# A two-block transformer on one core: more blocks beside the first feed-forward's rows, modulation units begun later, weighted squares on ScalarE

## The reference

```python
mod = c_act @ w_ada[l] + b_ada[l]                       # 6 * 2048 values
sh_a, sc_a, gt_a, sh_f, sc_f, gt_f = split(mod, 6)
...
x = x + gt_a * mix                                      # mix = (...) @ w_o
h = _rmsnorm(x, norm_ffn[l]) * (1.0 + sc_f) + sh_f
gate, up = jnp.split(h @ w_gate_up[l], 2, axis=-1)      # 2 * 5632 columns
x = x + gt_f * ((jax.nn.silu(gate) * up) @ w_down[l])
return _rmsnorm(x, final_norm)                          # end of the first block
# second block
h = rms_norm(x, pre_mix_g[l])
proj = h @ w_in[l]
```

## Time and profile before

| | us |
|---|---|
| median of 3 runs | 2901.99 (2901.83 to 2907.34) |
| the profiled execution | 2915.39 |
| its span, first to last instruction | 2912.6 |
| PE busy | 2802.3 (96%) |
| DVE busy | 2045.2 (70%) |
| ACT busy | 1316.2 (45%) |
| POOL busy | 209.4 (7%) |

### The profile page before, as it was taken

One profiled execution on the slowest core, in us unless ns is written; L12 is line 12 of the kernel. 1 busy time (PEld: TensorE's weight loads), 2 busy tenths in 40 slices (PEclk: granted clock), 3 DMA queues, 4 the chain that ended last, 5 costly groups with the idle time before them and its releaser, 6 DMA issues.

```text
span 2912.6 us, 45616 instructions
## 1 busy us (share of the span) xinstructions
PE 2802.3 (96%) x18282; PEld 2512.9 (86%) x18282; DVE 2045.2 (70%) x3021; ACT 1316.2 (45%) x2033; POOL 209.4 (7%) x180
## 2 busy tenths in 40 slices
PE   6988999999999999999999999999999999999997
PEld 6987788999999888888888889888888888888886
DVE  7888885667687786555555688997557566565665
ACT  4445542332344544444444454344555444444454
POOL 0230000000001100000000080111110000000001
PEclk9999999999999999999999999999999999999999
DMA  9863255555688587555555555544445555555553
GB/s 392 315 217 130 95 171 177 189 188 180 206 311 280 198 296 243 182 188 187 188 186 183 188 174 174 167 152 137 146 131 177 185 187 188 182 187 188 187 187 126
DMA packets 158466, 565.40 MB, mean 194 GB/s; under 512 B 17584, under 2 KB 21936, under 8 KB 158256
## 3 DMA queue, kind: packets, MB, share of 16 engines
q1 hardware_dynamic: 158256, 562.50, 57.9%
HBM read 560.33 MB, written 2.10 MB: 193 GB/s over the span
## 4 chain that ended last, share of the span: by engine, by line
PE 84%; DVE 10%; ACT 3%; issue 2%; DMA 1%; SPq 0%; POOL 0%; DVEq 0%; ACTq 0%; POOLq 0%
PE BK L346 32%; PE BK L347 16%; PE BK L349 10%; PE BK L351 9%; PE BK L350 9%; DVE LO L623 2%; PE BK L431 2%; DVE ADA L619 1%; ACT HI L507 1%; DVE B L673 1%; DVE TV L718 1%; DVE B L830 1%; PE BK L356 1%; PE BK L474 1%; PE BK L479 1%
## 5 line engine op out<-in xcount | busy, mean ns | idle before, releaser
L346 PE MATMUL BK<-H,HI 128*128 128x512 f32 x4144 | 1466.3, 399 | 10.8 <-DVE LO L623 7.6
L507 ACT ACTIVATE HI<-RAW 128x1024 fp32r<-128x1024 f32 x825 | 874.1, 1060 | 1287.7 <-PE BK L347 721.9
L623 DVE TENSOR_TENSOR LO<-RAW,HI 128x1024 fp32r<-128x1024 f32 x825 | 1018.1, 1235 | 402.0 <-ACT HI L507 399.8
L347 PE MATMUL BK<-H,LO 128*128 128x256 f32 x4144 | 1162.8, 281 | 0.0
L346 PEld LDWEIGHTS BK<-H,HI 128*128 128x128 f32 x4144 | 780.4, 188 | 205.9 <-DVE LO L623 9.2
L349 PE MATMUL BK<-H,HI 128*128 128x256 f32 x2720 | 809.3, 298 | 35.3 <-DVE B L673 20.3
L347 PEld LDWEIGHTS BK<-H,LO 128*128 128x128 f32 x4144 | 784.2, 189 | 0.2
L350 PE MATMUL BK<-H,HI 128*128 128x256 f32 x2720 | 778.3, 286 | 0.0
L351 PE MATMUL BK<-H,LO 128*128 128x256 f32 x2720 | 777.9, 286 | 0.0
L349 PEld LDWEIGHTS BK<-H,HI 128*128 128x128 f32 x2720 | 530.0, 195 | 76.6 <-issue 36.7
L350 PEld LDWEIGHTS BK<-H,HI 128*128 128x128 f32 x2720 | 530.7, 195 | 1.5 <-issue 1.0
(11 more groups left out here) (234 smaller groups left out, 1693.6 us busy)
## 6 DMA issues: line engine op xcount, KB each, us to landing
RAW<-wst_dram SPq DMA_DIRECT2D x825, 512.0 KB, 3.4
RAW<-wada_dram SPq DMA_DIRECT2D x155, 512.0 KB, 4.5
EARLY<-wada_dram SPq DMA_DIRECT2D x37, 512.0 KB, 8.5
EARLY<-wst_dram SPq DMA_DIRECT2D x33, 512.0 KB, 6.8
X<-xT_dram SPq DMA_DIRECT2D x8, 512.0 KB, 8.9
B<-bias_dram SPq DMA_DIRECT2D x32, 128.0 KB, 3.4
out_dram<-X SPq DMA_DIRECT2D x3, 512.0 KB, 2.7
CN<-consts_dram SPq DMA_DIRECT2D x1, 840.0 KB, 9.0
```

Source lines behind the costliest of these rows:

```text
L346: e.matmul(bk[:, :], hh, H[:, k, :], start=first, stop=False, skip_group_check=True)
L347: e.matmul(bk[:, 256:512], ll, H[:, k, 0:256], start=False, stop=last, skip_group_check=True).then_inc(S["tile"], 1)
L507: e.activation(HI[:, u % NHL, :], raw_at(slot), ACT.Copy).then_inc(S["hi"], 1)
L623: e.tensor_tensor(LO[:, u % NHL, :], raw_at(slot), HI[:, u % NHL, :].bitcast(f32), sub).then_inc(S["lo"], 1)
```

## The change

Three edits. `first1` runs three pairs, six blocks, in place of two pairs. The A units after the 160th are due at 160 + (i - 238) * 3/4 in place of 160 + (i - 220) * 5/8, so they stand between L240 and L281 in place of L222 and L272. `scaled_square` is one ScalarE operation (Square with final_norm as scale) that writes SQ's second half, or ACC2 for row 0, and `scaled_add` on GpSimd adds it to ACC2.

```diff
--- before.py
+++ after.py
@@ -529,6 +529,10 @@
                 q.wait_ge(ready, free)
                 e.activation(dst, src, ACT.Square).then_inc(S["st_a"], 1)
 
+            def scaled_square(dst, j, x, free, before):
+                q.wait_ge(x, free, before)
+                e.activation(dst, X[:, j, :], ACT.Square, scale=col("final_norm", j)).then_inc(S["st_a"], 1)
+
             def gained(dst, src, scale, ready):
                 q.wait_ge(ready)
                 e.activation(dst, src, ACT.Copy, scale=scale).then_inc(S["ev_a"], 1)
@@ -592,7 +596,7 @@
                 e.activation(y, t, ACT.Tanh).then_inc(S["cv_a"], 1)
 
             walk(dict(c_sigmoid=c_sigmoid, hi=hi, copy_sum=copy_sum, split_hi=split_hi, tanh=tanh, sigmoid=sigmoid, square=square,
-                      gained=gained, root_table=root_table, root_guess=root_guess, sine=sine, beta=beta, softplus=softplus, gate_exp=gate_exp, row_square=row_square,
+                      gained=gained, scaled_square=scaled_square, root_table=root_table, root_guess=root_guess, sine=sine, beta=beta, softplus=softplus, gate_exp=gate_exp, row_square=row_square,
                       soft_exp=soft_exp, turned=turned, g_exp=g_exp, g_copy=g_copy, conv_square=conv_square, conv_tanh=conv_tanh))
 
         def vector(e):
@@ -865,15 +869,9 @@
                 q.wait_ge(square, free)
                 e.tensor_tensor(SQ[:, 0, :], SQ[:, 0, :], B3[:, 6 + p, :], add).then_inc(S["st_g"], 1)
 
-            def scaled_square(j, x, free, before, at):
-                q.wait_ge(x, free)
-                sq = SQ[:, 1, :]
-                e.tensor_scalar(sq, X[:, j, :], col("final_norm", j), None, mult).then_inc(S["st_g"], 1)
-                q.wait_ge(("st_g", at + 1), before)
-                e.tensor_tensor(ACC2 if j == 0 else sq, sq, sq, mult).then_inc(S["st_g"], 1)
-                if j:
-                    q.wait_ge(("st_g", at + 2))
-                    e.tensor_tensor(ACC2, ACC2, sq, add).then_inc(S["st_g"], 1)
+            def scaled_add(square, before):
+                q.wait_ge(square, before)
+                e.tensor_tensor(ACC2, ACC2, SQ[:, 1, :], add).then_inc(S["st_g"], 1)
 
             def bias_mask(i, loaded):
                 q.wait_ge(loaded)
@@ -883,7 +881,7 @@
                 q.wait_ge(copied)
                 e.tensor_tensor(dst, dst, t, add).then_inc(S["ev_g"], 1)
 
-            walk(dict(part_add=part_add, square_add=square_add, scaled_square=scaled_square, bias_mask=bias_mask))
+            walk(dict(part_add=part_add, square_add=square_add, scaled_add=scaled_add, bias_mask=bias_mask))
 
         def walk(mine, log=None):
             w = Walk(mine)
@@ -904,7 +902,7 @@
             put = 16 * GROUPS
             late_at = len(kinds) - 16
             for i in range(ERA * (GROUPS - 1), N_TILES // 8):
-                due = min(N_ADA, put if i < 80 else 64 + (i - 80) * 3 // 4 if i < 208 else 160 + (max(i, 220) - 220) * 5 // 8)
+                due = min(N_ADA, put if i < 80 else 64 + (i - 80) * 3 // 4 if i < 208 else 160 + (max(i, 238) - 238) * 3 // 4)
                 kinds += ["L"] + ["A"] * max(0, due - put)
                 put = max(put, due)
             lin_at = [i for i, k in enumerate(kinds) if k == "L"]
@@ -1872,8 +1870,8 @@
                     yield from blocks(H1, h_tok, 0, "w_gate_up", 0, [o], wide=True)
 
             def first1(f_tok):
-                run(blocks(H1, h_tok, 0, "w_gate_up", 0, up1_outs(0, 0, f_tok) + up1_outs(1, 1, f_tok), wide=True))
-                return 2
+                run(blocks(H1, h_tok, 0, "w_gate_up", 0, [o for i in range(3) for o in up1_outs(i, i, f_tok)], wide=True))
+                return 3
 
             h2_free = [mid]
             ST = Stats(Sp.done)
@@ -1888,7 +1886,8 @@
                     yield from f(bk, tok, own)
                     if ci < 2:
                         return
-                    acc2[0] = do("scaled_square", "st_g", j, x_tok[j], ST.before, acc2[0], n=3 if j else 2)
+                    k = do("scaled_square", "st_a", SQ[:, 1, :] if j else ACC2, j, x_tok[j], ST.before, acc2[0])
+                    acc2[0] = do("scaled_add", "st_g", k, acc2[0]) if j else k
                     ST.before = ST.before + [acc2[0]]
                     yield
                     u_tok2[j] = yield from split(H1, j, X[:, j, :], x_tok[j], [fp_tok, h1_done[0]], scale=FP[:, j:j + 1])
```

## The result

The change made the kernel slower. In runs taken in turns on one chip the changed kernel took 2923.41 us (median of 9, 2911.93 to 2929.77), the kernel before 2901.58 (median of 9, 2896.86 to 2917.62). The ratio is 1.0065 with a 95% interval of 1.0049 to 1.0082: some 19 us (the two medians differ by 21.8), where 9 were forecast. The sign was right. The time lies above the forecast's range, which ended at 2917.

A forecast was written before the change was run, and what follows sets the result against it. TensorE was taken as the bound, 84% of the chain of waits. −1.3 at the start of the first feed-forward and +10.1 in the third w_down pass made +8.8 on 2901.99: 2911 us, range 2901 to 2917.

The forecast's parts named there:

- Part 1, the rows: Start of the first feed-forward, beside the norm's rows: moving modulation units leaves two TensorE waits, 2.2 us lost against 9.1 before.
- Part 1, the later units: The moved modulation units up to L281, during the evacuation: costed at nothing, since VectorE fits in 2.82 us per unit.
- Part 2: Six blocks in the first feed-forward: bank wait 2.1 us, late lo after forced evacuation 2.7, clock 0.8.
- Part 3: Third w_down pass: ScalarE's weighted square waits for GpSimd's square_add, holding its queue; +9.1 in the loop, +1.0 at row 15.
- four figures: Third w_down pass: queue loop per row without the added wait, 14.9 us for four rows; 22.4 with it, TensorE 19.5.
- The 0.42 ahead of the memset: End of the third w_down pass: VectorE's wait before the padding memset, subtracted from row 15's +1.4 to give +1.0.
- rival C: Third w_down pass and its end: fewer GpSimd operations free VectorE, part 1 gives 4.8; −5 to −6, 2896.5 us; chance 0.07.
- B: Third w_down pass: ScalarE's added wait is hidden, only row 15 and part of the loop count; 2902 to 2905; chance 0.25.
- D: First feed-forward and third w_down pass: waits bring three or more unhidden low clock stretches of 1.64; over 2916; chance 0.08.

The follow-up runs named there:

- e7: The changed kernel, with VectorE's operation for each of the last 32 modulation units on 128 of 1024 columns, loads whole; 2916.40 us, one execution.
- e8: The changed kernel, with each of the last 32 modulation units loading 128 of 1024 columns, VectorE's operations whole; 2914.16 us, one execution.
- e4: The changed kernel with the later modulation units at the old rate, 5 for 8, from the new start; 2914.80 us, ratio 1.0025 to the kernel before.
- e10: e9 plus the weighted square on ScalarE, waiting only for the addition of the row before; 2896.55 us against 2902.29 of the kernel before.
- e9: e6 with the convolution's padding memset issued in the second w_down pass; 2899.11 us against 2902.29 of the kernel before.
- e6: The kernel before with five blocks and the last 32 modulation units from L236 at 5 for 8; 2897.68 us against 2905.35 of before.
- e5: The kernel before with four blocks kept and the last 32 modulation units from L234 at 5 for 8; 2903.02 us against 2905.35 of before.
- e1: The changed kernel, with ScalarE's weighted square not waiting for the same row's square_add; 2913.56 us against 2907.19 of the kernel before.
- e3: The kernel before with six blocks and the later modulation units, squares on GpSimd as before; 2914.56 us, ratio 1.0020 to the kernel before.
- e12: The kernel before, unchanged, run and traced once more; 2906.74 us, one execution.

## Why the prediction was right or wrong

**Part 1, the rows: right.** Two waits of 1.2 and 0.95 were foretold, 1.07 and 0.74 found, and no low stretch ahead of tile 96 (−4.6 there).

**Part 1, the later units: wrong, and this is the step that failed.** It reads "I cost them at nothing: VectorE has ... some 2.5 of 2.82". The sum was of VectorE alone. It didn't count the loads, though each A unit is one load of 512 KB, the same as a weight unit. The changed mix needs 7 loads in four units of TensorE, 4 × 2.773 = 11.1 us: one each 1.58 us, 331 GB/s. The old one needs 13 in eight, 22.2 us: one each 1.71, 307 GB/s. The windows view of the changed kernel and, below it, of the kernel before:

```profile
1076.00:1096.00 20.00, 20.00 (x122) 17.67 (x121) 16.46 (x23) 9.12 (x14) 0.00 (x0) 1.00 0.94 333
1040.00:1147.00 107.00, 102.42 (x585) 88.02 (x583) 87.08 (x107) 48.03 (x71) 0.00 (x0) 1.00 0.86 304
```
```profile
20.00:60.00 40.00, 33.47 (x202) 30.62 (x202) 34.76 (x39) 21.16 (x37) 0.00 (x0) 0.87 1.03 409
...
1060.00:1100.00 40.00, 40.00 (x233) 34.99 (x232) 34.59 (x42) 19.28 (x29) 0.00 (x0) 1.00 0.91 314
```

Over the whole stretch the changed kernel moves 304 GB/s. For 20 us at a time it gets 333, and the DMA engines gave 409 at the start of the kernel, where on average 8.6 loads are under way and not 2.8. So it isn't that the engines can't carry more. Here there are five slots, and their turn is what counts. From the 58 loads that the changed kernel issues between 1040 and 1140: a load lands 4.9 us behind its issue (mean), and 3.8 later its slot is issued again, when `hi` and `lo` (1.06 + 1.22 and their waits) are through. A turn of 8.7 for five is 1.75 a load, over 1.58. TensorE shows the same: once the `lo`s have no lead left (they then end 0.1 us before their unit is due) it waits once in four units (at 1112.07, 1124.19 and 1136.28), so four units and their 7 loads take 12.1 us in place of 11.1, 1.73 a load. In e7 the turn is 5.8 + 2.7: with the slots given back at once more loads are in flight, and each lands later. In e8 it is 3.2 + 5.0, and TensorE's pace sets the turn. At 5 for 8 a load each 1.71 is asked, also a little more than the turn gives: by my estimate some 2 us are lost in 50 loads, which the lead and the stop of 1.8 for each `mod_sum` cover. At 3 for 4 it is 1 us in four units, and the lead is used up at once; the waits begin at 1051. The Trainium skill, in "Perfetto Trace Analysis", section "Engine Utilization", gives 358 GB/s as a core's share of HBM when both cores of a pair use it, and some 435 as the bound of its 16 DMA engines. By these figures 331 GB/s would have fitted, and the 333 over 20 us agrees; the measured turn decides, and over the whole stretch it didn't fit.

The price: 4.7 in waits, 3.4 in clock, and what is left of the +9.8, 1.7, in the pipeline's refill behind the six waits, some 0.3 each. The forecast did name the place ("Without that cover each late one would cost ..., in SyncE's loads"), at up to 1.19 each, but it gave it no chance and no count, and the sum took nothing of it, although the row with a DMA share of 0.91 can be read from the trace of before.

**Part 2: right in mechanism and near in size.** Bank 2.03 (2.1), `lo` 2.41 (2.7), one low stretch of 3.4 us, which costs 1.7 (the forecast took 0.8, half of one). By tile 120 parts 1 and 2 stand at −0.45, where −1.3 was foretold. How near this comes is in part chance: e4 had waits of 2.03 and 2.31 in the same places and no low stretch, and stands at 49.49 there, 2.1 under before.

**Part 3: right.** The new operation waits 1.3 to 1.6 in 14 of 16 rows, starts 1.73 behind the square, rows come 5.56 apart, TensorE waits inside the pass and for 6.15 at its end. Foretold +10.1, found +11.5, of which 1.1 is clock. Four rows of the loop take 22.23, where 22.4 were foretold. Its four figures (4.3, 4.2, 3.1, 3.2) don't follow from the counts beside them: a `lo` in two rows of four and a `hi` in three give 4 × 2.22 + 2 × 1.14 + 3 × 0.97 = 14.1, not 14.9. In the changed kernel a `lo` stands in three of the four, so the figures were right and the count wasn't. Two terms were off. The 0.42 ahead of the memset did not vanish: it is 0.43 after, and the profile now gives "issue" as its cause, so it was hardly TensorE that VectorE waited for in the earlier trace rows. And the longer waits brought a low stretch of 10.2 us, which costs a further 1.3 behind narrow tile 16.

The Trainium skill, in "SBUF — State Buffer", section "Who interferes with whom", has a VectorE operation with both inputs in SBUF and a GpSimd one that reads SBUF exclude each other. The traces agree in one direction: `square_add` took 1.20 over a `lo` and 0.72 with none. What would follow in the other, a relief of VectorE once two of three GpSimd operations are gone, was rival C; e10 against e9 puts it at the 0.3 above.

**The rivals.** B asked for a hidden wait, C for a relief: neither was there. D, the worse case, was right on the clock (20.4 us at 1.2 GHz in the feed-forward, 10.2 before), but its main cause, the loads, was in no rival. The range was too narrow because a term with a cost of nothing had no upper end.

**What stays open:** how what e7 gives back divides between VectorE's own time and slots that come free sooner; and why e6 is 0.28% faster with five blocks and e5 only 0.08% with four. Both reach tile 456 in their traces 7 us sooner than before, which is 0.24%. In these traces e5 is also at the slower of two paces for longer (section "What the runs showed of the hardware"), which makes 4.6 us; whether that was so in the other executions isn't shown.

## What to carry to other kernels

When work is moved to a denser place, sum every resource it takes there: its loads and the turn of their slots (from issue to landing to reissue) against what the trace shows there, not only the engine that computes. A wait put into an in-order queue costs its length for everything behind it, each time round the loop, so a cheap operation that waits for a slow engine can be dearer than the dear one that it replaces; where it can wait for something older, it cost 0.2 us in a pass of 88. Blocks beside each other are paid in banks: leave one free for the block that comes next.

## What the runs showed of the hardware

**Two paces at the same granted clock.** Wide tiles come either 2.826 or 2.773 us per unit of eight, for hundreds of microseconds, with TensorE never waiting and a granted clock of 1.00. The group of wide matmuls, 1200 to 1600, kernel before and e1:

```profile
L346 PE MATMUL BK<-H,HI 128*128 128x512 f32 x1133 | 400.5, 399 | 0.0
```
```profile
L346 PE MATMUL BK<-H,HI 128*128 128x512 f32 x1154 | 400.2, 391 | 0.0
```

From the `lo` of unit 290 to that of 462 before, its repeat, the change, e3, e5 and e7 have the slow one (486.95 us), e1 the fast one (477.82), others both. The change and e1 have the same code up to there. In all traces the pace changed only where TensorE also stood or slowed for a moment (behind a wait, at a `mod_sum`, between the first two blocks of a `w_down` pass), and held in between, for up to 89 units. e12 was to show whether the pace belongs to the kernel. From 290 to 462 it has the first trace's again, but in tiles 56 to 80 before has the slow pace and its repeat, the same kernel, the fast one, so the kernel alone doesn't fix it. It makes 9 us of difference between kernels with the same code there, as large as the effects under study. I don't know its cause.

**Low stretches after short waits.** TensorE fell to 1.2 GHz behind waits of 1.95 and 1.84 (before), behind 2.03 and 2.41 in a row, and behind 0.89 with four waits of 0.5 to 1.5 in the 85 us ahead of it; it did not behind 1.62 (before), nor behind 1.23 and 0.74 (e6). The length of a wait alone doesn't decide it: e1 and e4 both have 2.03 and 2.31 in a row in the same places, and only e1 fell.

**A VectorE memset has some 0.4 us of idle time ahead of it** in before (0.42), after (0.43), and in e9, where it stands in another pass (0.4).
